# A two-layer attention decoder on one core: early products for the output projection's first token tile, and rotary swaps issued by SP

## The reference, cut to what matters

```python
def apply_rope(x, cos, sin):
    x1, x2 = jnp.split(x, 2, axis=-1)
    return x * cos + jnp.concatenate([-x2, x1], axis=-1) * sin
...
def nsa_mixer(x, w_in, ...):        # 16 heads in 4 groups, head size 64
    proj = x @ w_in
    ...
    q_rot = apply_rope(q, cos, sin)
    k_slc = apply_rope(kv_heads(ks), cos, sin)
    k_win = apply_rope(kv_heads(kw), cos, sin)
    ...
        return gc[..., 0:1] * o_c + gc[..., 1:2] * o_s + gc[..., 2:3] * o_w
    ...
    return out @ w_o
def fox_mixer(x, w_in, b_f, w_o):
    ...
    return o.transpose(0, 2, 1, 3).reshape(B, S, HQ) @ w_o
def reference(x, ...):
    for i in range(DEPTH):          # DEPTH = 2
        y = nsa_mixer(...) if i % N_MIXERS == 0 else fox_mixer(...)
        x = layer_norm(ALPHA * x + y, ln1_g[i], ln1_b[i])
        f = conv_ffn(x, ffn_w_up[i], ffn_conv_w[i], ffn_conv_b[i], ffn_w_down[i])
        x = layer_norm(ALPHA * x + f, ln2_g[i], ln2_b[i])
```

## Time and profile before

| | |
|---|---|
| median of three runs (lowest to highest) | 1456.05 us (1453.08 to 1458.66) |
| profiled execution, its own time | 1452.71 us |
| its span, first to last instruction | 1450.9 us |
| PE busy | 1370.0 us (94%) |
| DVE / ACT / POOL busy | 694.5 / 670.4 / 622.1 us |
| mean granted TensorE clock | 0.985 |
| NSA units, group 3 | about 311.5 to 373.5 us |
| FoX pair 7 | about 1007 to 1024.5 us |

### The profile page before, as it was taken

One profiled execution on the slowest core, in us unless ns is written; L12 is line 12 of the kernel. 1 busy time (PEld: TensorE's weight loads), 2 busy tenths in 40 slices (PEclk: granted clock), 3 DMA queues, 4 the chain that ended last, 5 costly groups with the idle time before them and its releaser, 6 DMA issues.

```text
span 1450.9 us, 20004 instructions
## 1 busy us (share of the span) xinstructions
PE 1370.0 (94%) x7050; PEld 1123.9 (77%) x7050; DVE 694.5 (48%) x1312; ACT 670.4 (46%) x1249; POOL 622.1 (43%) x402
## 2 busy tenths in 40 slices
PE   8979888887999999999999899998899999999997
PEld 6857676666788888888888787887688888888886
DVE  3346666667284443442007577878284443442005
ACT  4356666666434444443123567777334444443210
POOL 2356666664434444444444222222334444444441
PEclk9999999989999999999999999999999999999999
DMA  9431211110423333334232313121422333324221
GB/s 279 98 73 52 44 52 45 52 45 1 156 77 88 101 89 99 101 91 141 88 102 75 95 49 86 46 75 59 158 75 81 105 90 101 99 89 139 94 73 58
DMA packets 170237, 127.59 MB, mean 88 GB/s; under 512 B 24032, under 2 KB 155860, under 8 KB 170164
## 3 DMA queue, kind: packets, MB, share of 16 engines
q1 hardware_dynamic: 167220, 121.38, 28.7%
q10 hardware_dynamic: 2944, 5.25, 1.4%
HBM read 116.98 MB, written 4.39 MB: 84 GB/s over the span
## 4 chain that ended last, share of the span: by engine, by line
PE 74%; DVE 14%; issue 3%; ACT 3%; DMA 3%; POOL 2%; ACTq 1%; SPq 0%; DVEq 0%; POOLq 0%
PE ps L919 14%; PE ps L921 14%; PE ps L920 14%; PE ps L1161 7%; PE ps L1163 7%; PE ps L1160 7%; PE ps L1081 2%; PE ps L1095 2%; DVE ptl L1434 2%; DVE xt L1574 2%; ACTq L635 1%; DVE negmax L1417 1%; DMA work<-work 1%; DVE xt L1564 1%; DVE stats L1568 1%
## 5 line engine op out<-in xcount | busy, mean ns | idle before, releaser
L429 POOL TENSOR_TENSOR wl<-raw,wh 128x1024 fp32r<-128x1024 f32 x180 | 436.7, 2430 | 674.5 <-ACT wh L548 674.3
L919 PE MATMUL ps<-xh,wh 128*128 128x512 f32 x968 | 392.0, 405 | 0.0
L921 PE MATMUL ps<-xh,wl 128*128 128x512 f32 x968 | 379.1, 392 | 0.0
L920 PE MATMUL ps<-xl,wh 128*128 128x512 f32 x968 | 378.0, 390 | 0.0
L548 ACT ACTIVATE wh<-raw 128x1024 fp32r<-128x1024 f32 x192 | 201.7, 1052 | 214.3 <-PE ps L1163 199.4
L921 PEld LDWEIGHTS ps<-xh,wl 128*128 128x128 f32 x968 | 182.2, 188 | 39.2
L919 PEld LDWEIGHTS ps<-xh,wh 128*128 128x128 f32 x968 | 184.2, 190 | 32.1 <-issue 0.2
L920 PEld LDWEIGHTS ps<-xl,wh 128*128 128x128 f32 x968 | 183.0, 189 | 32.1
L1595 DVE SCALAR_TENSOR_TENSOR work<-ps,conv,work 128x511 f32<-128x511 f32 x88 | 66.0, 750 | 221.9 <-ACT work L799 156.2
L662 ACT ACTIVATE prob<-ps,negmax 128x128 f32<-128x128 f32 x192 | 101.2, 527 | 93.4 <-DVE negmax L1417 78.3
L1564 DVE SCALAR_TENSOR_TENSOR xt<-xt,ps 128x512 f32<-128x512 f32 x32 | 20.5, 682 | 255.1 <-PE ps L1163 254.8
(11 more groups left out here) (192 smaller groups left out, 2092.2 us busy)
## 6 DMA issues: line engine op xcount, KB each, us to landing
raw<-in_ffn_w_up SPq DMA_DIRECT2D x88, 512.0 KB, 3.8
raw<-in_ffn_w_down SPq DMA_DIRECT2D x44, 512.0 KB, 3.4
raw<-in_fox_w_in SPq DMA_DIRECT2D x24, 512.0 KB, 4.0
raw<-in_nsa_w_in SPq DMA_DIRECT2D x12, 512.0 KB, 6.0
xt<-in_x SPq DMA_DIRECT2D x8, 512.0 KB, 6.2
raw<-in_nsa_w_in SPq DMA_DIRECT2D x16, 256.0 KB, 4.7
raw<-in_nsa_w_o SPq DMA_DIRECT2D x8, 512.0 KB, 4.1
raw<-in_fox_w_o SPq DMA_DIRECT2D x8, 512.0 KB, 3.5
```

The source lines that it names most:

```text
L429: nc.gpsimd.tensor_tensor(wl[:, slot, :, :], raw[:, slot, :, :], wh[:, slot, :, :].bitcast(F32), ALU.subtract).then_inc(s_wl, 1)
L919: nc.tensor.matmul(o, ah, bh, start=start, stop=False)
L920: nc.tensor.matmul(o, ah, bl, start=False, stop=False)
L921: return nc.tensor.matmul(o, al, bh, start=False, stop=stop)
```

## The change

Three things are changed.

1. The swap copies and the doubling of the keys are issued by SP. SP's program, which had been loads alone, now issues the copies of item n - 6 ahead of the load of item n (`item_moves`), and the last six of them ahead of the first six loads of the NSA output projection.
2. The first token tile's products with chunks 0 to 3 of both output projections are taken out of `down_pe` (its chunk-by-chunk loop runs over tiles 1 to 3) and put, half a bank pair at a time, between the units of NSA group 3 (`NSA_EARLY`: step: (chunk, half)) and of FoX pair 7 (`FOX_EARLY`, the eighth half after the last unit). Each half is three matmuls of 512 columns.
3. For this, chunks 2 and 3 must be split earlier: two `hi` on ACT and six `lo_part` on POOL in the first two windows of group 3, two `hi` on ACT in pair 7 (POOL's `lo` follow them).

```diff
@@ constants @@
+OUT_AT = (1, 0, 3, 2)
+NSA_EARLY = {2: (0, 0), 6: (1, 0), 12: (2, 0), 18: (3, 0), 21: (0, 1), 24: (1, 1), 27: (2, 1), 30: (3, 1)}
+FOX_EARLY = {1: (0, 0), 2: (1, 0), 3: (0, 1), 4: (1, 1), 5: (2, 0), 6: (2, 1), 7: (3, 0)}
@@ SP @@
-            for g in range(GROUPS):
...
+            def swap_halves(n):
+                rn, k = n - (n + 2) // 4, n % 4
+                src = tmpf if k == 0 else qf[n // 4 % 2][:, k - 2, :]
+                q = HD // 2
+                sp.wait_ge(s_pf, n + 1)
+                if rn:
+                    sp.wait_ge(s_r2, rn)
+                for b in range(4):
+                    sp.dma_start(swapped[b * q:(b + 1) * q, :], src[(b ^ 1) * q:((b ^ 1) + 1) * q, :]).then_inc(s_sr, 16)
+            def double_keys(g):
+                par = g % 2
+                sp.wait_ge(s_pl, 4 * g + 1)
...
+            for n in range(6):
+                load_item(n)
...
+            for n in range(6, NSA_ITEMS):
+                item_moves(n - 6)
+                load_item(n)
@@ SP, load_out @@
                 for k in range(KB):
+                    if c0 == C_WO0 and k < 6:
+                        item_moves(NSA_ITEMS - 6 + k)
                     load_down(c0 + k, w, k)
@@ POOL @@
-                    if g < GROUPS - 1 and w in (5, 6, 7):
+                    if 4 * g + v // 8 < NSA_ITEMS - 2 and w in (5, 6, 7):
                         lo_part(4 * (g + 1) + v // 8 + 6, 3 * (w - 5), min(3 * (w - 4), KB))
-            los(C_WO0 + 2, C_FOX + 4 - (C_WO0 + 2))
+            los(C_WO0 + R, C_FOX + 4 - (C_WO0 + R))
@@ ACT: swap_halves, double_keys and their calls are gone @@
-                    if g < GROUPS - 1 and w == 4:
+                    if u // 8 < NSA_ITEMS - 2 and w == 4:
                         c = 4 + 4 * (g + 1) + v // 8
                         hi(c + 2, (c + 2) % R)
...
-                for k in range(2, KB):
+                for k in range(R, KB):
                     hi_at(c0, k)
...
-                    if more and v in (0, 2, 5):
+                    if v in (0, 2, 5)[:3 if more else 2]:
                         hi_at(C_FOX, 3 * (pair + 1) + (0, 2, 5).index(v) + 2)
@@ PE @@
+            def down_half(c, k, m, h, src_h, src_l, at, start, stop):
+                hi_w, lo_w = (w[:, c % R, :, :].rearrange("p k c -> p (k c)")[:, h * 512:(h + 1) * 512] for w in (wh, wl))
+                a_h, a_l = (a[:, k, at[m] * P:(at[m] + 1) * P] for a in (src_h, src_l))
+                return mm3(ps[:, 2 * m + h, :], a_h, a_l, hi_w, lo_w, start, stop)
+            def first_tile(c0, oh, ol, heads, k, h):
+                if not h:
+                    pe.wait_ge(s_wl, c0 + k + 1)
+                pe.wait_ge(s_ol, heads + 2 * k + 2)
+                down_half(c0 + k, k, 0, h, oh, ol, OUT_AT, k == 0, False)
...
+                    elif v in NSA_EARLY:
+                        if v == 2:
+                            pe.wait_ge(s_pf, NSA_ITEMS)
+                        if NSA_EARLY[v] == (0, 1):
+                            pe.wait_ge(s_cl, HEADS // 2)
+                        first_tile(C_WO0, oh, ol, 0, *NSA_EARLY[v])
...
-                down_pe(c0, KB, n, oh, ol, (1, 0, 3, 2), range(QT), bank_ready, block_ready, (0, 2))
+                down_pe(c0, KB, n, oh, ol, OUT_AT, range(1, QT), bank_ready, block_ready, (0, 2), range(1, QT))
...
+                    elif v in FOX_EARLY:
...
+                        first_tile(C_WO1, oh2, ol2, HEADS, *FOX_EARLY[v])
...
             fox_stages(7, 1, None, more=False)
+            first_tile(C_WO1, oh2, ol2, HEADS, 3, 1)
             fox_pv((NSA_UNITS + FOX_UNITS) // 2 - 1)
```

More of the change, by code:

```diff
@@ L323, in _, with item_moves, load_item @@
             wsv = w_nsa[:, D + 2 * KV:D + 6 * KV].rearrange("(k p) (two r) -> p k two r", p=P, two=2)
-            for g in range(GROUPS):
[L325 to L334, removed]
+            def swap_halves(n):
[10 more added lines that the diff above has]
+                sp.wait_ge(s_pl, 4 * g + 1)
+                sp.dma_start(ks[par][HD:P, :, :].bitcast(F32), ks[par][0:HD, :, :].bitcast(F32)).then_inc(s_sw[par], 16)
+                sp.dma_start(kw[par][0:HD, :, :].bitcast(F32), kw[par][HD:P, :, :].bitcast(F32)).then_inc(s_sw[par], 16)
+            def item_moves(n):
+                if n % 4 == 1:
+                    double_keys(n // 4)
+                else:
+                    swap_halves(n)
+            def load_item(n):
+                g, k, c = n // 4, n % 4, 4 + n
+                if k >= 2:
+                    load(c, c % R, cols(w_nsa, g * REP * HD + (k - 2) * P))
+                    return
+                r0 = (0, KV)[k]
+                sp.wait_ge(s_wl, c - (R - 1))
+                for b in range(2):
+                    sp.dma_start(raw[:, c % R, :, b * HD:(b + 1) * HD],
+                                 wsv[:, :, b, r0 + g * HD:r0 + (g + 1) * HD]).then_inc(s_raw[c % R], 16)
+            for n in range(6):
+                load_item(n)
+                if n == 3:
                     sp.wait_ge(s_vt, 6)
@@ L622, in item_copy @@
                     nc.scalar.activation(qf[g % 2][:, k - 2, :], ps[:, BP, :], ACT.Copy, scale=SCALE).then_inc(s_pf, 1)
[L624 to L635, removed]
             def item_hi(g, k):
@@ L686, in _ @@
             item_copy(0, 0)
-            swap_halves(0, 0)
             hi(7, 7 % R)
@@ L698, in _ @@
             item_hi(0, 1)
-            double_keys(0)
             item_copy(0, 2)
-            swap_halves(0, 2)
             hi(9, 9 % R)
@@ L705, in _ @@
             item_copy(0, 3)
-            swap_halves(0, 3)
             for g in range(GROUPS):
@@ L718, in _ @@
                         cmp_exp(u // 16 + 1)
-                    if w == 5 and turned and item[1] == 0:
-                        double_keys(item[0])
                     if g < GROUPS - 1 and w == 7:
@@ L724, in _ @@
                     unit_hi(u, w % 4)
-                    if g < GROUPS - 1 and w == 7 and v // 8 != 1:
-                        swap_halves(g + 1, v // 8)
                     if u % 16 == 0:
@@ L1164, in down_product, with down_pe @@
                 return last
-            def down_pe(c0, nk, n, src_h, src_l, at, order, bank_ready, block_ready, turn_banks):
+            def down_pe(c0, nk, n, src_h, src_l, at, order, bank_ready, block_ready, turn_banks, early=range(QT)):
                 for k in range(nk - R):
@@ L1170, in down_pe @@
                     pe.wait_ge(s_wl, c0 + k + 1)
-                    for m in (order if k == 0 else range(QT)):
+                    for m in (order if k == 0 else early):
                         if k == 0:
@@ L1319, in fox_stages @@
                             kstep(C_FOX + 3 * (pair + 1) + r, (C_FOX + 3 * (pair + 1) + r) % R, k, (BP, BX, BP)[r])
+                    elif v in FOX_EARLY:
+                        if v == 1:
+                            pe.wait_ge(s_pf, NSA_ITEMS + HEADS // 2)
+                        if v == 3:
+                            pe.wait_ge(s_pl, NSA_ITEMS + 3 * HEADS // 2)
+                        first_tile(C_WO1, oh2, ol2, HEADS, *FOX_EARLY[v])
                     if v % 2 and (v > 1 or not first):
```

5 lines of the change are left out of this document (removed).

## The result

The changed kernel took 1436.41 us (median of four runs, 1436.14 to 1436.59); the kernel before, beside it, 1454.57 (1452.70 to 1458.66). The ratio is 0.9871, with a 95% interval of 0.9851 to 0.9890: 18.8 us faster, where 1438 and 18 us had been forecast. The profiled execution has a span of 1434.8 us against 1450.9, with a mean clock of 0.987.

The account below looks back on a forecast made before the run. TensorE, busy 94% of the span, was taken as the bound: let it wait less or fill its waits. -9.7 - 3.8 - 4.2 = -17.7 from 1452.7 gives 1435.0; with the median 3.3 higher, forecast 1438, range 1430 to 1450.

Parts of the forecast that it names:

- Part one: Swap copies moved to SP, in NSA groups 0 to 2 and the prologue: -9.7 us in all.
- Landing: NSA groups 0 to 2: copies land some 1.7 us sooner, six TensorE waits behind DVE's sine product go, -5.3 us.
- ACT's stall and its clock: Second-head-pair starts: waits shrink without ACT's DMA issues, -3.6 us; the low clock after the 2.43 us wait goes, -1.6.
- Prologue: First swap queues on SP behind the loads of chunks 8 and 9, so it lands later: +0.8 us.
- Part two: Early products in NSA group 3: -5.6 projection, +2.1 exposure, +1.0 POOL, +0.2 hand-over, -1.5 clock; sum -3.8 us.
- Exposure: NSA group 3: what the eight halves cost where TensorE's waits do not hide them, +2.1 us (0 to 5.6).
- POOL's pieces: NSA group 3, first window: POOL's low halves of two more chunks delay TensorE, +1.0 us (0 to 2.7).
- Clock: NSA group 3: a shorter opening wait leaves less of the 1.2 GHz stretch from 316.50, -1.5 us (0 to -4.2).
- slower: Rival, 1462 us, chance 0.05: TensorE at 1.2 GHz where the halves stand, so a half costs 1.28 us.
- Part three: Early products in FoX pair 7: -5.6 projection, +0.4 exposed, +2.3 DVE beside POOL, -1.3 clock; sum -4.2 us.
- Work only moved: Rival, 1450 us, chance 0.12: TensorE pays each half in full, so the two -5.6 give nothing.
- Clean: Rival, 1430 us, chance 0.13: products hide wholly, clock holds at both low stretches, DVE misses POOL.

Follow-up runs that it names:

- the kernel with that alone: Against the kernel before: ACT still issues the copies, SP holds the next load until they land, no early products; 1449.15 us, ratio 0.9964.
- the kernel with filled waits: Changed kernel with NSA halves moved to steps 1 and 17 (two each), 21, 25, 29 and ahead of the last PV; 1429.98 us, ratio 0.9842.

## Why the prediction was right, point by point

**Part one (-9.7).** Right, term by term. *Landing* -5.3: the kernel with that alone gave 5.2. *ACT's stall and its clock* -3.6 and -1.6: the waits fell from 2.48 and 2.43 to 1.13 and 1.28, the low clock behind the second went, the third fell from 3.25 to 2.08. *Prologue* +0.8: the sine product came 0.6 later, the first scores behind it 0.5 (90.98 against 90.52). Swaps alone gave 10.5. In the trace of the changed kernel the stretch to group 3's mark, which leaves out the third ACT wait, gave 10.6 where these terms make 8.5; with the swaps alone it gave 8.1. The trace of the swaps alone has one sine product that still waits, 1.36 us at 292.26, and 3.4 us of low clock at 74.7, and the changed kernel's has neither. So the spread between traces is as large as any miss, and "term by term" holds for the waits and stretches named here, not to tenths of the sum. The rival *swaps no sooner* is out: the copies land in 2.0.

On the rule of the Trainium skill (DMA: Bandwidth & Descriptors, Queues, rings and completion order) I had put the prologue near +1: +0.5 does not contradict it, and the copies behind 1.5 MB (3.4 us after the last issue, against 1.97 behind 1 MB) agree with it.

**Part two (-3.8).** Here the sum failed, and other misses hid it. The output projection lost its 5.6 us (the stretch from it on shows 4.8, of which my hand-over explains 0.2), but group 3 grew by 3.9, where my terms had it grow by some 0.4 (2.1 exposed, 1.0 for POOL, less 1.5 of clock and 1.2 of the opening wait). Three terms:
- *Exposure* +2.1. I took the wait behind each half as cover in full. TensorE's waits shrank by no more than 2.8 of 5.6, so at least 2.8 was exposed. The halves stood beside short waits, and the three longest of the group (2.08, 2.09, 1.41) had none.
- *POOL's pieces* +1.0: neither shown nor refuted; 59.04 against 59.50, with 3.4 us less of low clock.
- *Clock* -1.5: nothing came back, 13.3 us low against 13.5 (6.8 to 13.7 in the four kernels with this placement). I held a wait of 2 us harmless, because the 2.09 before had led to only 3.25 us of low clock. The wait of 2.08 now led to 6.6, with the half of step 2 in it, and the 2.09 to 6.7, with that of step 18. In the three other kernels with this placement each of these waits led to 3.4 or 6.8 us, so the wait says that the clock may fall and not for how long. This is the mechanism of my rival *slower*, on two halves out of sixteen.

The prediction also said that group 3 would last about 1 us less, which its own terms don't give, and that growth of over 4 us would show it wrong; 3.9 is just short of that. Against nothing but the swaps, group 3 grew by 4.5, so NSA's part gave 1 us and not 3.8, as the kernel without it says too.

**Part three (-4.2).** Right in its mechanism: -7.0 behind the pair against -5.6 - 1.3, and +2.4 in it against 0.4 + 2.3. DVE's two scalings took 1.6 us each above those of 0.49 and 0.29, just over the 1.5 each that I had taken at most from the 1.83 of the earlier trace rows. The whole clock term came, 2.6 rather than the middle 1.3, and moving one half showed that it needs this half. About a third of it lay inside the pair before, so with the clock set apart the pair grew by 3.3 against 2.7 forecast, and the projection lost 5.2 against 5.6: the clock's surplus paid for that. The rule of the Trainium skill (SBUF — State Buffer, Who interferes with whom), that the later one is blocked for the whole of the other's instruction, agrees with the ends of the four rows; it cost less than the 2 x 2.4 that I had worked out from it, because each scaling met only the rest of a subtraction. That the splitting alone costs 3.8 us by the ratios was not foreseen: in its trace the clock adds to DVE's loss when nothing fills the waits.

**The rivals.** *Work only moved* holds for group 3 and is refuted for pair 7. *Clean* was not reached, but its 1430 is what the kernel with filled waits took.

**The total.** -17.7 was forecast; the ratio gives -18.8, the two traces -16.1. Parts one and three carried it. That the total came within 2 us is partly luck: part two came out some 3 us worse, and in the trace the stretch of the swaps 2 us better.

## What to carry to other kernels

When work is moved into the idle time of an engine, place it in the longest waits first and not beside many short ones: it must be issued just ahead of the instruction that waits, and one piece in a long wait can also keep the clock of what follows. Count the cover by the engine's summed waits, not by the wait behind each piece. A copy put on a queue of loads inherits the waits of the loads ahead of it: put it ahead of them.

## What the runs showed of the hardware that was not expected

- With 0.7 us of matmuls in a wait of 2.78 us TensorE stayed at 2.4 GHz behind it in six of seven traces, and ran 3.4 us at 1.2 GHz in the seventh; without them it was at 1.2 GHz for 6.8 us or more in all of seven. In group 3 one half in the wait of 2.08 was enough in both traces that have it.
- The same instructions in group 3 lasted 61.78, 62.62, 63.54 and 63.96 us in four kernels with the same eight halves there, at mean clocks of 0.94, 0.92, 0.89 and 0.89: where the clock falls varied between them (one execution of each). A difference of 2 us in such a stretch needs more than one trace. Why it varies stays open.
- DVE's 128 x 128 scaling took 0.29 us alone and 1.90 beside a subtraction on POOL, ending 0.09 after it.
- A swap of 64 KB pieces on SP's queue, issued behind 1 MB of loads, had landed 1.97 us after its last issue; behind 1.5 MB it took 3.4, and ahead of these loads 1.5.
